# Time mix of the even layer: two head pairs side by side instead of one after the other

## The reference

```python
    kk = heads(k * k_k)
    kk = kk / jnp.maximum(jnp.sqrt(jnp.sum(kk * kk, axis=-1, keepdims=True)), 1e-12)
    k = k * (1.0 + (a - 1.0) * k_a)
    rh, kh, vh, ah, wh = heads(r), heads(k), heads(v), heads(a), heads(decay)
    y = _rwkv7_scan(rh, wh, kh, vh, kk, ah)
    ...
    bonus = jnp.sum(rh * kh * r_k.astype(jnp.float32), axis=-1, keepdims=True) * vh
    y = (y + bonus.reshape(bsz, t, B_WIDTH)) * g.astype(jnp.float32)
```

```python
    A = jnp.where(strict, jnp.einsum("bhncd,bhnsd->bhncs", kb, kc) * decay, 0.0)
    sol = lax.linalg.triangular_solve(A, rhs, left_side=True, lower=True, unit_diagonal=True)
```

## Time and profile before

| what | value |
|---|---|
| median of 3 runs | 4620.15 us (4614.26 to 4620.54) |
| profiled execution, its own time | 4617.3 us |
| span of the profiled execution | 4615.5 us |
| TensorE matmul busy | 4050.1 us, 88% |
| VectorE busy | 1641.0 us, 36% |
| ScalarE busy | 1327.6 us, 29% |
| mean granted TensorE clock | 0.891 |
| time mix, from its first vector instruction to the first of `group_norm` | 323.4 us, 7% of the span |
| six inversions of the delta net | 42 us each |

### The profile page before, as it was taken

One profiled execution on the slowest core, in us unless ns is written; L12 is line 12 of the kernel. 1 busy time (PEld: TensorE's weight loads), 2 busy tenths in 40 slices (PEclk: granted clock), 3 DMA queues, 4 the chain that ended last, 5 costly groups with the idle time before them and its releaser, 6 DMA issues. The chain is left out here.

```text
span 4615.5 us, 55382 instructions
## 1 busy us (share of the span) xinstructions
PE 4050.1 (88%) x21416; PEld 3361.9 (73%) x21416; DVE 1641.0 (36%) x2889; ACT 1327.6 (29%) x2306; POOL 194.7 (4%) x160
## 2 busy tenths in 40 slices
PE   7997888997998887999786777999878879999998
PEld 5777776775777775787465655787655569999998
DVE  2365435233246434423335434332245421111112
ACT  2464523231256433322132222222223311111111
POOL 0141000000033000000000000000000000000000
PEclk9997779998998878999897878999986689999999
DMA  3100012221200001222110001222220014545443
GB/s 116 41 1 1 0 37 82 86 96 45 99 5 1 0 0 55 91 91 91 55 59 1 0 18 64 80 99 76 89 91 0 18 49 182 191 161 189 167 152 130
DMA packets 51453, 324.51 MB, mean 70 GB/s; under 512 B 6528, under 2 KB 7424, under 8 KB 20352
## 3 DMA queue, kind: packets, MB, share of 16 engines
q1 hardware_dynamic: 51328, 322.85, 19.4%
HBM read 319.68 MB, written 2.10 MB: 70 GB/s over the span
## 5 line engine op out<-in xcount | busy, mean ns | idle before, releaser
L491 PE MATMUL bank<-high 128*128 128x512 f32 x2480 | 980.7, 395 | 116.0 <-DVE low L585 81.1
L492 PE MATMUL bank<-low,high 128*128 128x512 f32 x2480 | 976.4, 394 | 0.0
L493 PE MATMUL bank<-high,low 128*128 128x512 f32 x2480 | 975.4, 393 | 0.0
L491 PEld LDWEIGHTS bank<-high 128*128 128x128 f32 x2480 | 473.0, 191 | 224.2 <-issue 67.3
L492 PEld LDWEIGHTS bank<-low,high 128*128 128x128 f32 x2480 | 473.6, 191 | 98.5
L493 PEld LDWEIGHTS bank<-high,low 128*128 128x128 f32 x2480 | 472.7, 191 | 99.6
L549 DVE TENSOR_TENSOR low<-weight_ring,high 128x2048 fp32r<-128x2048 f32 (+1 forms) x144 | 319.2, 2218 | 553.1 <-ACT high L506 553.1
L2860 PE MATMUL bank<-chosen,glu_ring 128*128 128x176 f32 x2816 | 422.0, 313 | 0.0
L2860 PEld LDWEIGHTS bank<-chosen,glu_ring 128*128 128x128 f32 x2816 | 420.1, 190 | 0.0
L506 ACT ACTIVATE high<-weight_ring 128x2048 fp32r<-128x2048 f32 (+1 forms) x144 | 266.6, 1852 | 269.1 <-PE bank L493 230.2
L2871 PE MATMUL bank<-hidden,down_ring 128*128 128x176 f32 x1408 | 211.3, 313 | 0.0
(11 more groups left out here) (465 smaller groups left out, 4972.9 us busy)
## 6 DMA issues: line engine op xcount, KB each, us to landing
glu_ring<-in_w_expert SPq DMA_DIRECT2D x88, 1024.0 KB, 4.8
weight_ring<-in_w_ff SPq DMA_DIRECT2D x64, 1024.0 KB, 5.2
down_ring<-in_w_expert_down SPq DMA_DIRECT2D x64, 704.0 KB, 5.1
weight_ring<-in_w_in SPq DMA_DIRECT2D x22, 1024.0 KB, 4.9
weight_ring<-in_w_ffe SPq DMA_DIRECT2D x22, 1024.0 KB, 4.8
weight_ring<-in_w_downe SPq DMA_DIRECT2D x16, 704.0 KB, 4.0
weight_ring<-in_w_ino SPq DMA_DIRECT2D x11, 1024.0 KB, 4.8
weight_ring<-in_w_ine SPq DMA_DIRECT2D x9, 1024.0 KB, 4.8
```

Of the source, the lines that this page charges most:

```text
L491: nc.tensor.matmul(mem.bank[b][:, :], whole, high[:, k, :], start=(k == 0), stop=False)
L492: nc.tensor.matmul(mem.bank[b][:, :], whole, low[:, k, :], start=False, stop=False)
L493: last = nc.tensor.matmul(mem.bank[b][:, :], rest, high[:, k, :], start=False, stop=(k == kt - 1))
```

## The change

`time_mix` takes two groups of two pairs instead of four passes of one pair; the hardware loop is gone and the code stands twice.

- `rwkv_prepare` does each step for pair 0 and then for pair 1. The norm is summed into 128x8 (squares as the stationary operand), Sqrt and RECIPROCAL run on 128x8 and 128x16, and the result is spread back by a ScalarE copy and four transposes for each pair. The staging copies of r, v and the decay and the three parameter copies go.
- `invert` serves 28 steps i (level and stream) with one semaphore of each kind. Product banks are 0 to 2 and turn banks 3 to 5, used in rotation (i mod 3), instead of two banks for each stream. A `turn` waits for `taken` and `joined`, a `clear` for `joined` and `taken` (`ended` in the last two steps). The late products, now eight items in banks 6 and 7, stand after every third step. This helper is used by the delta net too.
- `masked_product` alternates the two heads (lower and upper 64 partitions) from matmul to matmul.
- `rwkv_scan` holds two states for each pair, folds the decay into w and into a scaled copy of rho on ScalarE (`half_factor`, `factor`), updates the state in one instruction without waiting for the chunk's own output, and puts the outputs straight into `y`.

The core of the diff:

```diff
+    steps, lag, rotation = LEVELS * count, count // 2, 3
+    cleared = steps - count
...
+        product_bank = lambda i: mem.bank[i % rotation]
+        turn_bank = lambda i: mem.bank[rotation + i % rotation]
+        late_at = {} if late is None else {3 * (k + 1): k for k in range(late.items)}
...
+            def turn(i):
+                if i >= count:
+                    pe.wait_ge(taken, i - count + 1)
+                if i >= rotation:
+                    pe.wait_ge(joined, i - rotation + 1)
...
+            def clear(i):
+                n = i % count
+                pe.wait_ge(joined, i + 1)
+                before = i - rotation
+                if before >= cleared:
+                    pe.wait_ge(ended, before - cleared + 1)
+                elif before >= 0:
+                    pe.wait_ge(taken, before + 1)
...
+            for i in range(lag):
+                turn(i)
+            for i in range(steps):
+                if i < lag:
+                    turn(i + lag)
+                clear(i)
+                if lag <= i < steps - lag:
+                    turn(i + lag)
+                if i in late_at:
+                    late.multiply(pe, late_at[i], late_taken).then_inc(late_product, 1)
...
+def masked_product(nc, banks, left, right):
+    for t in range(TT):
+        for par in range(2):
+            c, lanes = slice(t * P, (t + 1) * P), slice(par * HEAD, (par + 1) * HEAD)
+            last = nc.tensor.matmul(banks[par][:, c], left[lanes, c], right[lanes, c], start=True, stop=True)
+    return last
...
-            dve.wait_ge(rooted, 1)
-            steps.did(nc.vector.tensor_scalar(scale[:, :], scale[:, :], 1e-12, None, ALU.max))
-            steps.settle()
-            steps.did(nc.vector.reciprocal(scale[:, :], scale[:, :]))
...
+            dve.wait_ge(rooted, 2)
+            steps.did(nc.vector.tensor_scalar(root[:, :, :], root[:, :, :], 1e-12, None, ALU.max))
+            steps.settle()
+            steps.did(nc.vector.reciprocal(root[:, :, :], root[:, :, :]), inverted)
...
+            for s in range(TT):
+                for p, j in pairs:
+                    if s == 0:
+                        pe.wait_ge(w_taken[p], TT - 1)
+                    else:
+                        pe.wait_ge(state_ready[p], s)
+                        for par in range(2):
+                            nc.tensor.matmul(pass_banks[p][par][:, 0:HEAD], w[lanes[par], p, s * P:(s + 1) * P],
+                                             state[lanes[par], p, (s - 1) % 2, :], start=True, stop=True) \
+                                .then_inc(passed[p], 1)
+                    if s >= 1 and p == 1:
+                        put_out(0, s - 1)
+                    if s >= 2 and p == 0:
+                        put_out(1, s - 2)
+                for p, j in pairs:
+                    if s < TT - 1:
+                        grow(p, s)
...
-    with nc.Fori(0, RW_PAIRS) as j, buffers(nc, v=[P, SEQ], factor=[P, TT], par=[P, len(VEC_J)],
-                                            more=[P, 8, SEQ]) as parts:
...
+    with buffers(nc, neg=[P, 4, SEQ], seen=[P, 2, 3, 2, SEQ], factor=[P, 2, 2, TT]) as (neg, seen, factor):
+        for group in range(RW_PAIRS // 2):
+            b = TimeMix(mem, u, group, neg, seen, factor)
+            rwkv_prepare(nc, mem, vec, u, decay, rate, b)
+            invert(nc, mem, b.neg, b.twice, [0, 0, 0, 0], MaskedProducts(nc, mem, b))
+            rwkv_scan(nc, mem, y, b)
```

More of the change, by code:

```diff
@@ L1390, in _ @@
         def _(dve):
[L1391 to L1399, removed]
@@ L1400, in _ @@
-            for n in range(count):
-                dve.wait_ge(product[n], LEVELS)
-                nc.vector.tensor_tensor(chunks(twice[:, n, :]), chunks(mem.bank[2 * n][:, :]), idents, ALU.add)
+            for i in range(steps):
+                l, n = divmod(i, count)
+                dve.wait_ge(turned, i + 1)
+                mask = mem.levels[:, upper[n], l, :].unsqueeze(1).broadcast_to([P, TT, P])
+                nc.vector.tensor_tensor(chunks(joint[:, n, :]), chunks(turn_bank(i)[:, :]), mask, ALU.mult) \
+                    .then_inc(joined, 1)
+                if i - lag in late_at:
+                    k = late_at[i - lag]
+                    dve.wait_ge(late_product, k + 1)
+                    late.take(k).then_inc(late_taken, 1)
@@ L1404, in _ @@
+            for i in range(cleared, steps):
+                dve.wait_ge(product, i + 1)
+                nc.vector.tensor_tensor(chunks(twice[:, i - cleared, :]), chunks(product_bank(i)[:, :]),
+                                        ident.unsqueeze(1).broadcast_to([P, TT, P]), ALU.add).then_inc(ended, 1)
         @block.tensor
         def _(pe):
-            def turn(l, n):
-                if l >= 1:
-                    pe.wait_ge(taken[n], l)
-                for c in slices:
-                    last = nc.tensor.transpose(mem.bank[2 * n + 1][:, c], matrix[:, n, c], ident)
-                last.then_inc(turned[n], 1)
@@ L1781, in take @@
[L1781 to L1801 removed]
+        self.nc, self.mem, self.b = nc, mem, b
@@ new lines, in _ @@
+            for p, j in pairs:
+                ends = by_chunk(b.about[p])[:, 0:TT - 1, P - 1]
+                steps.did(nc.vector.tensor_tensor(b.factor[:, p, 0:TT - 1], ends, by_chunk(b.run[p])[:, 1:TT, mid],
+                                                  ALU.add), factor_ready)
+            for p, j in pairs:
+                dve.wait_ge(spread, p + 1)
+                steps.did(nc.vector.tensor_tensor(b.kk[p], b.kk[p], sum_bank[p][:, :], ALU.mult), normed)
+            steps.settle()
```

503 lines of the change are left out of this document (269 added, 234 removed).

## The result

| | before | changed |
|---|---|---|
| median, first chip (4 runs each) | 4620.34 us (4614.26 to 4630.64) | 4497.07 us (4491.53 to 4504.48) |
| ratio, 95% interval | | 0.9736 [0.9719, 0.9752] |
| profiled execution, its own time / span | 4617.3 / 4615.5 us | 4491.5 / 4489.7 us |
| mean granted TensorE clock | 0.891 | 0.901 |
| time mix | 323.4 us | 212.7 us |

The forecast was 4526 us with a range of 4507 to 4558; the kernel is faster than its low end. Of the 125.8 us of span, 110.7 are in the time mix (forecast 91.0) and 15.1 outside it (forecast 0).

What follows compares the result with a forecast made beforehand. The prediction took each head pair as bound by a chain through three engines, none full. Its terms summed to 232.4 us for the time mix against 323.4, a gain of 91.0 from 4617.3: 4526.3 us, range 4507 to 4558.

Steps and rivals of the forecast that it cites:

- preparation, both groups: Time mix preparation: 25.5 us per group of two pairs in place of 37.3, range 24 to 29.
- inversion, both groups: Time mix inversion: 51.9 us per group in place of 79.0, from 41.3 four-stream, 3.6 and 7.0 for added items.
- borders and new code: Time mix: twelve phase borders become six, of 1.0 to 1.3 us; unlooped code costs at most about 1.8.
- scans, one of them slow: Time mix scans: 28.6 us per group at 2.4 GHz in place of 36.0, plus 12 for one slow scan.
- Delta net: 0: Delta net's six inversions: same instructions, each new wait follows from an older one, so no change in time.
- price of a slow scan: Time mix scan at 1.2 GHz: about 12 us more; one of the two scans counted as slow.
- B: Rival: alternating heads do not run at once in inversion and preparation; 20 us more, 4546 to 4558; chance 0.12.
- C: Rival: overlap fails in preparation and scan because VectorE's single queue holds both pairs; gives back 38 us, 4565; chance 0.08.
- D: Rival: TensorE's queue pays for second waits, 392 places in eight inversions; 4593 or 4655 us; chance 0.06, half of it slower.
- E: Rival: phases do as forecast, but something not in the trace of before eats over 60 us; chance 0.04.

Runs made afterwards that it cites:

- r3: The kernel before with the new inversion (six rotating banks, two waits) in the delta net alone, time mix untouched: 4616.32 us, ratio 0.9983.
- r1: The changed kernel again, unaltered, on a second chip with a profile of its own: 4512.12 us, ratio 0.9761 to the kernel before.
- r4: The changed kernel with both heads' masked product written head after head in place of alternating: 4507.10 us, ratio 0.9739.
- r10: The changed kernel without the redundant second waits of turns and of clears on the copies: 4499.09 us, ratio 0.9743.
- r6: The changed kernel with the two heads alternating from matmul to matmul in the chunk outputs of both scans: 4458.90 us, ratio 0.9655.

## Why the prediction was wrong, and where it was right

The sum against the profiled executions:

| term | forecast | measured | difference |
|---|---|---|---|
| preparation, both groups | 51.0 | 46.9 | -4.1 |
| inversion, both groups | 103.8 | 105.1 | +1.3 |
| borders and new code | 8.4 | 5.6 | -2.8 |
| scans, one of them slow | 69.2 | 55.1 | -14.1 |
| everything outside the time mix | 0 | -15.1 | -15.1 |

Two terms, the delta net and the scans, carry nearly all of the miss, 15.1 and 14.1 us; with either of them right the kernel would have come out inside the range.

**Delta net: 0.** This step failed. For the inversion it holds to 0.1 us. But I had looked only at whether the new waits cost something inside the phase, and named no work that comes behind it. The last clear's wait for `ended`, which I priced at 0.1 us, moves TensorE's last work 0.5 us towards the border, and the scans behind gained 13.7 us in the profile, 2 to 13 by timing (r3), because their clock fell less. The row that could have told was there: the earlier trace rows had the same recurrence at 1.00 and at 0.58. I used it for the price of a slow scan in the time mix and not to ask what sets the clock in the delta net. These rows also start behind the solve, and so hide that the first scan, which I took as one at 2.4 GHz, had run its first 7 us at 1.2 GHz: it lasted 28.2 us, where the changed kernel has scans of 25.0.

**Scans.** This is the second step that failed, by its sizes: the list of the work was right. The solve took 6.6 us (2500.82 to 2507.41) and not 8.9: I had taken matmuls at the low clock at its start, and the clock did not fall. Growths take 0.23 a pair, not 0.6, and first outputs 0.49, not 1.0; I priced these two as head by head, although the growths do alternate, as the forecast said. The later outputs are 1.88 and the one stall is 0.48, as forecast. So a scan at 2.4 GHz is 24.3 and not 28.6. The price of a slow scan was near: r1's first scan, at a clock of 0.53, took 39.5 with its border, 14.4 more than the 25.1 at 2.4 GHz, against 12. Which scans are slow was a draw, as counted: scans and their borders took 56.7 us in the first profile and 69.8 in r1, forecast 71.8. That the sum for r1 nearly fits is luck: both of its scans fell, and that made up for the sizes.

**Preparation** 23.5 and 23.4, just under the low bound of 24 to 29: TensorE's last turn ends at 2442.71, 3 us ahead of the phase, so it does not become the bound that I feared. **Inversion** 52.8 and 52.3 against 51.9: steps of 1.33 as forecast, and an item that costs 1.29 between its neighbours where I took 1.15. **Borders** 0.8 to 1.1; code written twice instead of looped cost nothing visible.

**Rivals.** B fell on the item of 1.09; r4, where the heads do stand one after the other, shows that its price was half of what I wrote. C fell, since preparation and scan overlap too. D fell twice, by the steps of 1.33 and by r10. E fell with the time mix of 212.7 us, in which nothing new of that size appears. The range was too narrow at its low end because it held no term for the clock outside the time mix, and because four of the five terms were off on the same side.

## What to carry to other kernels

Where the granted clock swings at phase borders, price TensorE's pause at the border and not only the phase: 0.5 us less pause went with 8 us here, and idle transposes in the shadow of another engine's last work gave 28 us in the old kernel and 14 to 26 in the new one. Write matmuls that use different halves of the array alternately, also when they accumulate into the same bank and only the columns differ. And when a change brings in one template of the kernel (here the alternating heads), look at once where the kernel still goes without it: r6 gained 37 to 49 us by it, where the change had gained 110 to 122.

## What was not expected of the hardware

- TensorE's clock fell to 1.2 GHz at the border behind pauses of 1.83 us and more in 27 of 30 delta scans, behind unfilled ones of 1.58 in 10 of 24, and behind filled ones of 1.14 to 1.58 in none of 30.
- Four matmul records on alternating 64-column halves, all with 128 rows, start and pass in 0.27 us, the same as two records of one half. Head after head, two sets of eight records on different 64-row halves took 1.64 us, between the 1.09 of full overlap and 2.18.
- Taking 48 second waits out of each inversion (r10) changed neither its steps of 1.33 us nor, beyond the intervals, the time.
- Executions of one kernel differ by 10 to 20 us and more (4613.6 to 4636.2 for the kernel before, 17 runs). The one kernel with two profiles shows where it can come from: they are 11.0 us apart, and the time mix, by the clock that its two scans were granted, 12.4.
